# Condition sums of block 2 one stage forward: into the two feed-forwards, none left in the joint projection

## What is computed

```python
def first_block(x, ...):
    for layer in range(2):
        h = rms_norm(x, norm_mix_pre[layer])
        h = neighbourhood_attention(h, ...) if layer == 0 else dilated_attention(h, ...)
        x = x + rms_norm(h, norm_mix_post[layer])
        h = rms_norm(x, norm_ffn_pre[layer])
        x = x + rms_norm(swiglu(h, w_gate, w_up, w_down), norm_ffn_post[layer])
    return x

def second_block(x, c, ctx, c_ctx, ada_w, ada_b, w_in, ...):
    mod = jnp.split(silu(c) @ ada_w[0] + ada_b[0], 6, axis=-1)
    modc = jnp.split(silu(c_ctx) @ ada_w[0] + ada_b[0], 6, axis=-1)
    sh1, sc1, g1, sh2, sc2, g2 = mod
    u = concat([layernorm(ctx) * (1 + sc1c) + sh1c, layernorm(x) * (1 + sc1) + sh1])
    mix = token_mixer(u, w_in, ...)                     # begins with u @ w_in
    x = layernorm(DN_ALPHA * x + g1 * mix[own tokens], ln1_w, ln1_b)
    h = layernorm(x) * (1 + sc2) + sh2
    return layernorm(DN_ALPHA * x + g2 * moe_ffn(h, ...), ln2_w, ln2_b)
```

## Time and profile before

| what | value |
|---|---|
| runs (3) | 2023.73 us median, 2023.27 to 2025.92 |
| profiled execution | 2027.24 us, of which the span from first to last instruction is 2025.1 |
| busy | PE 1870.4 us (92%), DVE 979.9 (48%), ACT 647.1 (32%), POOL 331.1 (16%) |
| chain that ended last | PE 83%, DVE 7%, DMA 4%, ACT 3% |
| loads of a feed-forward item | 1024 KB, 4.7 to 5.6 us from issue to landing (median by weight) |
| row loads | 48 of 512 KB, median 4.7 us |

### The profile page before, as it was taken

The page is one execution under the profiler, slowest core; times in us unless marked ns, Lnnn a source line. Parts: engine busy times, 40 slices in busy tenths (PEclk is TensorE's granted clock), DMA queues, the critical chain, the costliest instruction groups (busy, mean ns, idle before and its releaser), DMA issues.

```text
span 2025.1 us, 33529 instructions
## 1 busy us (share of the span) xinstructions
PE 1870.4 (92%) x14234; PEld 1342.9 (66%) x14234; DVE 979.9 (48%) x1446; ACT 647.1 (32%) x1012; POOL 331.1 (16%) x316
## 2 busy tenths in 40 slices
PE   7989998999997999899999789979999999999981
PEld 6878998989997999765756679874333333333320
DVE  5745555465664677746545754663222222222116
ACT  5544334444454433420033532421211111211110
POOL 2100000000000100012200024402233333333413
PEclk9989999999998999999888789979999999999996
DMA  8534555544443877446596000075999999999995
GB/s 278 189 105 157 187 186 186 164 146 147 150 143 119 298 249 249 148 148 186 170 338 231 1 14 4 3 296 184 397 371 369 375 372 369 365 377 378 373 400 201
DMA packets 199700, 456.76 MB, mean 226 GB/s; under 512 B 32982, under 2 KB 154326, under 8 KB 170000
## 3 DMA queue, kind: packets, MB, share of 16 engines
q1 hardware_dynamic: 157104, 377.18, 51.6%
q0 software_dynamic: 35712, 58.00, 8.5%
q10 hardware_dynamic: 6752, 19.67, 2.7%
HBM read 549.91 MB, written 52.43 MB: 297 GB/s over the span
## 4 chain that ended last, share of the span: by engine, by line
PE 83%; DVE 7%; DMA 4%; ACT 3%; issue 2%; POOL 1%; SPq 0%; ACTq 0%; POOLq 0%; DVEq 0%
PE psum L349 33%; PE psum L3467 15%; PE psum L3451 7%; PE psum L1570 7%; PE psum L1577 2%; PE psum L3393 2%; PE psum L2607 2%; DMA mem<-in_exp_w_dram 2%; DMA mem<-in_exp_w_dram,mem 1%; PE psum L2591 1%; ACT w_hi L405 1%; PE psum L3480 1%; DVE w_lo L410 1%; PE psum L3150 1%; PE psum L569 1%
## 5 line engine op out<-in xcount | busy, mean ns | idle before, releaser
L410 DVE TENSOR_TENSOR w_lo<-mem,w_hi 128x2048 fp32r<-128x2048 f32 x122 | 279.3, 2292 | 229.5 <-ACT w_hi L405 226.9
L349 PE MATMUL psum<-x_hi,w_hi 128*128 128x256 f32 x1216 | 349.3, 287 | 4.5 <-DVE x_lo L556 4.5
L3467 PE MATMUL psum<-mem 128*64 128x512 f32 x1536 | 344.0, 601 | 8.8 <-DMA mem<-in_exp_w_dram,mem 7.5
L349 PE MATMUL psum<-x_hi,w_lo 128*128 128x256 f32 x1216 | 344.3, 283 | 0.0
L349 PE MATMUL psum<-x_lo,w_hi 128*128 128x256 f32 x1216 | 343.4, 282 | 0.0
L405 ACT ACTIVATE w_hi<-mem 128x2048 fp32r<-128x2048 f32 x122 | 233.8, 1918 | 193.7 <-PE psum L349 190.5
L3467 PEld LDWEIGHTS psum<-mem 128*64 128x64 f32 x1536 | 106.9, 138 | 207.4 <-issue 194.8
L349 PEld LDWEIGHTS psum<-x_hi,w_hi 128*128 128x128 f32 x1216 | 233.6, 192 | 10.2 <-DVE w_lo L410 4.8
L349 PEld LDWEIGHTS psum<-x_lo,w_hi 128*128 128x128 f32 x1216 | 237.2, 195 | 0.7
L349 PEld LDWEIGHTS psum<-x_hi,w_lo 128*128 128x128 f32 x1216 | 236.2, 194 | 0.0
L3451 PE MATMUL psum<-mem 128*64 128x512 f32 x768 | 175.3, 598 | 1.2 <-DVE mem L3553 1.2
(11 more groups left out here) (512 smaller groups left out, 2858.5 us busy)
## 6 DMA issues: line engine op xcount, KB each, us to landing
mem<-in_exp_w_dram SPq DMA_DIRECT2D x192, 1024.0 KB, 10.1
mem<-in_dil_w_qkv_dram SPq DMA_DIRECT2D x36, 1024.0 KB, 5.3
mem<-in_ada_w_dram POOLq DMA_DIRECT2D x48, 512.0 KB, 4.7
mem<-in_ffn_w_gate_dram SPq DMA_DIRECT2D x22, 1024.0 KB, 5.6
mem<-in_ffn_w_up_dram SPq DMA_DIRECT2D x22, 1024.0 KB, 5.5
mem<-in_ffn_w_down_dram SPq DMA_DIRECT2D x22, 1024.0 KB, 4.7
mem<-in_w_in_dram SPq DMA_DIRECT2D x13, 1024.0 KB, 5.5
mem<-in_na_w_qkv_dram SPq DMA_DIRECT2D x12, 1024.0 KB, 8.6
```

The costliest lines, as they stand in the source:

```text
L349: ins = pe.matmul(out, lhs[a], rhs[b], start=start and k == 0, stop=stop and k == 2, **kw)
L410: dve.tensor_tensor(w_lo[n % SLOTS][:, 0, :], ring[:, n % SLOTS, :], w_hi_f[n % HI][:, 0, :], ALU.subtract).then_inc(S("w_split"), 1)
L3467: ins = pe.matmul(psum[r, up, :].rearrange("p (a n) -> p a n", a=2), xg[:, b % 2, c, x * P + 64 * e:x * P + 64 * e + 64], w_up[s][e][:, :, ...
```

## The change

The sums for sh1 and sc1 move from the second feed-forward to the first, and those for the other four vectors from the joint projection to the second feed-forward. The accumulators and row buffers of the first are used again for the second, cleared by POOL in between. In the second feed-forward four rows of 512 KB are taken behind each tile (in the loop), where two rows with two takes each were. The final sums of the four vectors use two PSUM banks in turn with DVE's additions between, instead of five banks at once. ACT's loads for block 2 stay in the second feed-forward, as `block2_loads`; `modT`, which holds the results, gets a place that lives through both blocks.

```diff
-    tail = [("mod2", 0), ("gla_end", 0), ("ssd_pre", 0), ("conv", 0), ("conv", 1), ("ssd_pre", 1), ("conv", 2),
+    tail = [("gla_end", 0), ("ssd_pre", 0), ("conv", 0), ("conv", 1), ("ssd_pre", 1), ("conv", 2),
             ("ssd_pre", 2)] + [("conv", j) for j in range(3, 9)]
...
-        experts_pe(pe, "ff0", N_FF)
+        experts_pe(pe, "ff0", N_FF, mod_pe)
+        pe.wait_ge(*at("mod_done", MOD_DONE))
         rms_turn_pe(pe, 6)
...
-        experts_pe(pe, "ff1", N_FF, mod_pe)
+        experts_pe(pe, "ff1", N_FF, mod2_pe)
...
-        experts_dve(dve, "ff0", N_FF, FF0)
+        experts_dve(dve, "ff0", N_FF, FF0, mod1_take)
+        mod_dve(dve)
         for n in range(EARLY):
             lo_dve(dve, DIL_QKV + n)
...
-        experts_dve(dve, "ff1", N_FF, FF1, mod1_take, ctx_rows_dve)
-        mod_dve(dve)
+        experts_dve(dve, "ff1", N_FF, FF1, mod2_take, ctx_rows_dve)
+        mod2_dve(dve)
         residual_dve(dve)
...
+    mod_acc = dict(zip(MOD_2, [mod1_acc[:, j, v, :] for j in range(2) for v in range(2)]))
     N_ROWS = len(MOD_2) * KC
 
-    def mod2_row(pool, h):
+    def mod2_pool(pool):
+
         W = d["ada_w_2"][0].rearrange("(p c) n -> p c n", p=P)
-        j, c = MOD_2[h // KC], h % KC
-        if h >= 2:
+        pool.wait_ge(*at("mod_done", len(MOD_SUMS)))
+        link(pool, "pool", pool.memset(mod1_acc.rearrange("p j v n -> p (j v n)"), 0.0))
+        for h in range(N_ROWS):
+            i, j, q = h // 8, MOD_2[h // 2 % 4], h % 2
             pool.wait_ge(S("mod_used"), N_ROWS1 + h - 1)
-        pool.dma_start(mod_rows[h % 2], W[:, c, j * D:(j + 1) * D]).then_inc(S(f"mod_rows{h % 2}"), 16)
...
+            pool.dma_start(mod1_rows[:, q, :], W[:, 2 * i + q, j * D:(j + 1) * D]).then_inc(S(f"mod_rows{q}"), 16)
+
+    def mod2_take(dve, i, m):
+        acc2 = mod_acc[MOD_2[m]]
+        for q in range(2):
+            dve.wait_ge(S(f"mod_rows{q}"), 64 * i + 16 * (N_ROWS1 // 2 + m + 1))
+            dve.scalar_tensor_tensor(acc2, mod1_rows[:, q, :], silu_c[:, bass.ds(2 * i + q, 1), 0], acc2, ALU.mult, ALU.add
+                                     ).then_inc(S("mod_used"), 1)
+            dve.wait_ge(S("mod_used"), 8 * i + (N_ROWS1 + 2 * m + q + 1))
+
+    MOD2_ROWS = [(j, g, h) for j, g in ((2, g1_b), (5, g2_b)) for h in range(2)]
 
     def mod2_pe(pe):
         pe.wait_ge(S("mod_used"), N_ROWS1 + N_ROWS)
-        for j, b in ((2, 0), (5, 2)):
-            for h in range(2):
-                pe.matmul(bank(b + h), C("ones"), mod_acc[j][:, 512 * h:512 * h + 512], start=True, stop=True)
+        for n, (j, g, h) in enumerate(MOD2_ROWS):
+            if n >= 2:
+                pe.wait_ge(S("mod2_rows"), n - 1)
+            pe.matmul(bank(2 + h), C("ones"), mod_acc[j][:, 512 * h:512 * h + 512], start=True, stop=True
+                      ).then_inc(S("mod_sums"), 1)
+        pe.wait_ge(S("mod2_rows"), 3)
         for m, j in enumerate((3, 4)):
             for c in range(KC):
-                ins = pe.matmul(bank(4, 1, 8 * m + c), mod_acc[j][:, c::KC], C("ones")[:, 0:1], start=True, stop=True)
+                ins = pe.matmul(bank(2, 1, 8 * m + c), mod_acc[j][:, c::KC], C("ones")[:, 0:1], start=True, stop=True)
         ins.then_inc(S("mod_sums"), 1)
```

More of the change, by code:

```diff
@@ L88, in weave_order @@
 def weave_order(steps, j_rw, jobs):
-    order, gla, rows = [], 0, 0
+    order, gla = [], 0
     def step():
@@ L100, in weave_order @@
                 order.append(("move", m - 1))
-                for _ in range(2):
-                    if rows < 32:
-                        order.append(("row", rows))
-                        rows += 1
             if gla < steps and (m >= 6 or (part == 1 and m >= 1)):
@@ L117, in weave_order @@
             order.append(("half", 2 * m + 1))
-        if m == j_rw:
-            while rows < 32:
-                order.append(("row", rows))
-                rows += 1
         order += tail[:3]
@@ L318, in program @@
     ada_cols = alloc(6, KC)
+    modT = alloc(6, 2, KC)
     base_top = top[0]
@@ L386, in program @@
     X_NO = {"na": 0, "wo0": 8, "ff0": 10, "dil": 18, "wo1": 26, "ff1": 28, "wo2": 36}
-    HI_NO = {"wo0": 0, "wo1": 2}
+    HI_NO = {"wo0": 0, "wo1": 11}
     def x_part(pe, key, c):
@@ L1299, in block1_act @@
         rms_hi_act(act, gains[:, 2, :], 0)
+        mod1_act(act)
         experts_act(act, "ff0", N_FF, FF0)
@@ L1316, in block1_act @@
         rms_hi_act(act, gains[:, 3, :], 0)
-        mod1_act(act)
+        block2_loads(act)
         experts_act(act, "ff1", N_FF, FF1, ctx_root_act)
@@ L1355, in block1_pool @@
         na_pool(pool)
+        pool.wait_ge(S("x_split"), X_NO["ff0"] + KC)
+        mod1_pool(pool)
         pool.wait_ge(S("x_split"), X_NO["dil"] + KC)
@@ L1360, in block1_pool @@
         pool.wait_ge(S("x_split"), X_NO["ff1"] + KC)
-        mod1_pool(pool)
+        mod2_pool(pool)
     TILES = ALL // P
@@ L1372, in program @@
     g2_b = alloc(D)
-    modT = alloc(6, 2, KC)
     z_tok = alloc(NT, 512)
@@ L1412, in mod1_act, with block2_loads @@
         act.wait_ge(S("mod_in"), 16 * 3)
+        act.activation(silu_c.rearrange("p k v -> p v k"), c_in, ACT.Silu).then_inc(S("mod_silu"), 1)
+    def block2_loads(act):
         act.dma_start(ctx_tok, d["ctx_2"][0].rearrange("(t p) c -> p t c", p=P)).then_inc(S("stage_in"), 16)
@@ L1419, in mod1_act @@
             act.dma_start(dst, d["ada_b_2"][:, g * D:(g + 1) * D].to_broadcast([P, D])).then_inc(S("mod_in"), 16)
-        act.activation(silu_c.rearrange("p k v -> p v k"), c_in, ACT.Silu).then_inc(S("mod_silu"), 1)
     def mod1_pool(pool):
@@ L1465, in mod_dve @@
         ins.then_inc(S("mod_done"), 1)
-    mod_rows = [aT[:, 4 * q:4 * q + 4, :].rearrange("p c t -> p (c t)") for q in range(2)]
-    mod_acc = {2: xn[:, 0, :], 5: xn[:, 1, :], 3: gain_b, 4: hid.rearrange("p a b -> p (a b)")}
+    mod_acc = dict(zip(MOD_2, [mod1_acc[:, j, v, :] for j in range(2) for v in range(2)]))
     N_ROWS = len(MOD_2) * KC
-    def mod2_row(pool, h):
+    def mod2_pool(pool):
         W = d["ada_w_2"][0].rearrange("(p c) n -> p c n", p=P)
-        j, c = MOD_2[h // KC], h % KC
-        if h >= 2:
+        pool.wait_ge(*at("mod_done", len(MOD_SUMS)))
+        link(pool, "pool", pool.memset(mod1_acc.rearrange("p j v n -> p (j v n)"), 0.0))
+        for h in range(N_ROWS):
+            i, j, q = h // 8, MOD_2[h // 2 % 4], h % 2
@@ L1496, in mod2_pe @@
+        pe.wait_ge(S("mod2_rows"), 3)
         for m, j in enumerate((3, 4)):
             for c in range(KC):
-                ins = pe.matmul(bank(4, 1, 8 * m + c), mod_acc[j][:, c::KC], C("ones")[:, 0:1], start=True, stop=True)
+                ins = pe.matmul(bank(2, 1, 8 * m + c), mod_acc[j][:, c::KC], C("ones")[:, 0:1], start=True, stop=True)
         ins.then_inc(S("mod_sums"), 1)
     def mod2_dve(dve):
-        dve.wait_ge(S("mod_sums"), 1)
-        for g, b in ((g1_b, 0), (g2_b, 2)):
-            dve.tensor_tensor(g, g, banks(b, 2), ALU.add)
@@ L1505, in mod2_dve @@
-        dve.tensor_tensor(modT[:, 3, 0, :], ada_cols[:, 3, :], bank(4, KC), ALU.add)
-        dve.scalar_tensor_tensor(modT[:, 4, 0, :], bank(4, KC, 8), 1.0, ada_cols[:, 4, :], ALU.add, ALU.add)
+        dve.wait_ge(S("mod_in"), 16 * 8)
+        for n, (j, g, h) in enumerate(MOD2_ROWS):
+            dve.wait_ge(S("mod_sums"), n + 1)
+            gh = g[:, 512 * h:512 * h + 512]
+            dve.tensor_tensor(gh, gh, bank(2 + h), ALU.add).then_inc(S("mod2_rows"), 1)
+        dve.wait_ge(S("mod_sums"), 5)
@@ L1509, in program @@
+        dve.tensor_tensor(modT[:, 3, 0, :], ada_cols[:, 3, :], bank(2, KC), ALU.add)
+        dve.scalar_tensor_tensor(modT[:, 4, 0, :], bank(2, KC, 8), 1.0, ada_cols[:, 4, :], ALU.add, ALU.add
+                                 ).then_inc(S("mod2_rows"), 1)
     top[0] = stage_top
@@ L1919, in mixed_pe @@
                 next(gla)
-            elif what == "mod2":
-                mod2_pe(pe)
             elif what == "ssd_pre":
@@ L1952, in mixed_dve @@
                 next(gla)
-            elif what == "row":
-                mod2_take(dve, n)
-            elif what == "mod2":
-                mod2_dve(dve)
             elif what == "gla_end":
@@ L1967, in mixed_pool @@
         gla = gla_pool(pool)
-        pool.wait_ge(S("item_used"), MOD)
-        for h in range(2):
-            mod2_row(pool, h)
         for what, n in ORDER:
@@ L1973, in mixed_pool @@
                 next(gla)
-            elif what == "row" and n + 2 < N_ROWS:
-                mod2_row(pool, n + 2)
     top[0] = stage_top
```

19 lines of the change are left out of this document (3 added, 16 removed).

## The result

The changed kernel took 2050.56 us (median of 4 runs, 2048.52 to 2051.23) where the kernel before took 2024.83 (median of 4, 2023.27 to 2029.17): a ratio of 1.0111, 95% interval 1.0085 to 1.0137. It is slower by some 22 us by this ratio, and by 25.7 us by the two medians: three times the forecast of 7.4 or more, and outside its range. The profiled execution's span is 2049.3 us, that of before 2025.1.

A forecast was written before the change was run, and what follows sets the result against it. PE was taken to bound the three stages touched. PE work and its queues (-13.3 + 6.2 + 7.9 = +0.8 us) plus 6.6 us of row stall gave +7.4 on 2023.73: 2031.1 us, range 2024.5 to 2038.

The forecast's parts named there:

- end of the first feed-forward: Residual there begins 11.1 instead of 4.95 us after the last up product, behind mod_pe and two queued splits: +6.2 us.
- row takes in the second feed-forward: In the tile loop, DVE waits for rows with the next gate's split queued behind, so PE waits: +6.6 us.
- end of the second feed-forward: There mod2_pe replaces mod_pe, +5.4 us, and half clock in the last down product costs 2.5: together +7.9 us.
- joint projection: This stage loses 10.8 us of PE sums and 2.5 us of half clock behind them: -13.3 us.
- x: Second feed-forward: time from issue of a tile's fourth row load to DVE's take of it, assumed 5.3 us.
- The mechanism: Second feed-forward: two buffers for four rows a tile make DVE wait mid-takes, delaying the split PE needs; 6.6 us.
- the formula: Second feed-forward: DVE's period per tile is 12.83 + x, exceeding PE's 17.06 us beyond x = 4.23.
- Rival 2: Second feed-forward: third and fourth row fall on a gate load, x 5.8 to 6.4, sum +11.4 to +16.2 us; chance 0.13.
- Rival 1: Second feed-forward: rows keep up, x under 4.8, stall 0 to 2.9 us, time 2024.5 to 2027.4; chance 0.20.
- Rival 3: Stage ends: the sums hide in waits PE has anyway, up to 19.6 us, down to 2011.5 us; chance 0.05.

The follow-up runs named there:

- e1: The changed kernel with four row buffers instead of two in the second feed-forward; ratio 1.0020 to the kernel before.
- e2: The changed kernel, still two buffers, with a tile's four takes split over two places of DVE's program; ratio 1.0014 to the kernel before.
- e3: The changed kernel without 30 of its 32 row loads in the second feed-forward, all products kept; ratio 1.0070, tiles 183.1 us.
- e4: The kernel before with only the shift and scale rows moved to the first feed-forward; ratio 1.0036 to the kernel before.
- e5: e1 without the 16 one-column products that sum the rows of kinds 3 and 4; ratio 1.0011 to the kernel before.
- e10: e2 with the one-column products moved behind the context's transposes, into PE's wait; ratio 0.9966 to the kernel before.
- e6: e1 with the one-column products moved behind the context's transposes, into PE's wait; ratio 0.9973 to the kernel before.

## Why the prediction was wrong

| step | forecast | measured |
|---|---|---|
| end of the first feed-forward | +6.2 | +6.0 |
| second attention | 0 | +2.9 |
| row takes in the second feed-forward | +6.6 | +17.7 |
| end of the second feed-forward | +7.9 | +8.4 |
| joint projection | -13.3 | -11.3 |
| sum | +7.4 | +23.7 |

**The step that failed is the size of x.** "The pair has no weight load beside it, and the 5.8 has one but no second row, so I take the middle, 5.3." It came out as 6.36, 1.1 us more. The mechanism was right, and so was the formula: in the tile shown above x is 6.15, which gives 18.98 us for the 18.96 measured. The seven periods from 710.68 to 844.98 are 19.19 us on average, from which 12.83 + x gives x = 6.36; read from issue to take, the fourth rows of these seven tiles have x from 5.3 to 8.2, 6.31 on average. With 17.06 for PE that is 7 x 2.13 = 14.9 us, and the first period with its x of 8.03 adds 20.86 - 17.06 - 0.9 = 2.9: 17.8, where the trace has 17.7. Every tenth of a microsecond in x counts seven times. e1, e2 and e3 show that the wait for the row is the whole of this cost, since each takes it away by other means.

The trace of before held a better value, hidden in the median of the earlier trace rows. Of the sixteen rows there, seven were asked for 1.0 us behind a gate load and landed in 5.8 to 6.2 us; the seven that came 2.5 to 2.6 us after them landed in 4.4 to 5.0. (The first two, asked for ahead of the loop, took longer, up to 12.2.) In the new place the third row of the tiles four to seven is asked for 1.4 us behind a gate load, and both rows landed in 5.7 to 6.1. The first three tiles were worse: there the third row goes out just ahead of the gate load and lands in 3.9 us, and the fourth, behind both, takes 6.8 to 8.1 to land. Tile two, from DVE's, POOL's and SP's timelines:

```profile
724.53 1.28 DVE L1485 SCALAR_TENSOR_TENSOR mem<-mem 128x1024 f32<-128x1024 f32 x1 [2.85 <-DMA mem<-in_ada_w_dram]
730.18 1.28 DVE L1485 SCALAR_TENSOR_TENSOR mem<-mem 128x1024 f32<-128x1024 f32 x1 [4.36 <-DMA mem<-in_ada_w_dram]
...
720.65 0.53 POOL L1479 DMA_DIRECT2D mem<-in_ada_w_dram  x1 [9.27 <-DVE mem L1485]
721.97 0.53 POOL L1479 DMA_DIRECT2D mem<-in_ada_w_dram  x1 [0.79 <-DVE mem L1485]
...
720.77 0.56 SPq L641 DMA_DIRECT2D mem<-in_ffn_w_gate_dram  x1
```

The upper end of the prediction's values, 6.4, would have come out nearly right, but partly by luck: it is the longest landing of another stage. No run changes the weight loads, so that the gate load is what lengthens x is read from these places in time and not shown by an experiment.

Rival 2 (third and fourth row fall on a gate load) is what the tiles did, at the top of its range and above. The argument against it, "as DVE falls behind, its takes move away from that load", was wrong. The load of the gate tile is released by an item of PE, PE waits for the split, and the split stands behind the takes. So from tile four to tile seven load and takes fall back together: the third row follows the gate load by 1.38 to 1.40 us each time.

Rival 1 (rows keep up) fell with it: the shortest of the 32 landings is 3.8 us and the median 5.7. The fit of the Trainium skill (DMA: Bandwidth & Descriptors, Anatomy of one DMA), 3.2 us as an estimate, is below every one of them.

**The second attention** was not in the sum. PE's wait at its first pair is as long as before, 2.3 us, but the half clock that follows was not there before (windows of the changed kernel, then of before):

```profile
414.00:416.00 2.00, 2.00 (x12) 2.00 (x10) 1.35 (x3) 1.47 (x2) 0.00 (x0) 0.50 0.96 334
416.00:418.00 2.00, 2.00 (x15) 2.00 (x15) 1.15 (x1) 0.82 (x1) 0.00 (x0) 0.76 0.00 0
```

```profile
406.00:408.00 2.00, 0.54 (x5) 0.55 (x6) 1.93 (x6) 0.00 (x0) 0.00 (x0) 1.00 0.70 193
408.00:410.00 2.00, 2.00 (x20) 2.00 (x19) 1.21 (x2) 1.96 (x2) 0.00 (x0) 1.00 0.99 340
```

1.5 us are lost here, 1.1 at the start of the output product, where 0.50 lasts longer, and the rest in the first products of the stage. I had charged half clock only behind the one-column products; that a plain shift of a stage can change its clock did not occur in any step. What decides where the clock falls stays open.

**The stage ends** were right. The first took 6.0 for 6.2: mod_pe with the two splits behind it on DVE, at a clock of 1.00 from 330 to 350 us, as the step had it for mod_pe's old place. At the second, e4 shows 5.4 us for mod_pe (forecast 5.5), e5 that the one-column products cost 7.8 and the clock 2.4 (forecast 2.5, taken between 0 and 5.6).

**The joint projection** lost 10.8 us of sums and the 2.5 of half clock as forecast, but in the changed kernel its own first products run at half clock for some 4 us, which takes some 2 us of that back (16.47 us for its first piece, 14.12 in e10 and before). In e6 and e10, where the clock is at 1.00 when this piece starts, the stage shrank by 13.2 and 12.8. Rival 3 had its place right in part: PE has a wait at the end of the second feed-forward, not ahead of the last down product but behind it. With the 7.8 us of one-column products in that wait the end of the stage takes 23.4 us, and 22.0 without them (e5), so e6 and e10 hide some 6.4 of the 7.8. That was not what this change does.

## What to carry to other kernels

A load that can only be asked for when the buffer's last use ends is on the path in full, from issue to landing. Take its price from the loads that were asked for at the same distance from the same traffic, one by one: a median over a stage mixes loads with different neighbours, and here the middle between two quieter values was 1.1 us short, seven times over. If an engine's work must wait for such a load, look first at what stands behind it in the engine's program: splitting the takes over two places of the loop was worth as much as doubling the buffers. One-column sums, in which the clock fell as well, belong into a wait of the bound engine that is there anyway. And when a stage moves in time, its half-clock stretches may fall elsewhere: here the second attention took 1 to 3.5 us longer, without any edit in it.
